# Down projection of a decoder's SwiGLU as seven block products instead of eight, one core of Trainium2

## The reference

```python
h = _rmsnorm(x, g_fp)
f = (jax.nn.silu(h @ w_g) * (h @ w_u)) @ w_d      # w_g, w_u: 1024 x 2816, w_d: 2816 x 1024
x = x + _rmsnorm(f, g_fq)
```

## Time and profile before

| | |
|---|---|
| median of 3 runs | 1484.61 us (1484.59 to 1484.89) |
| profiled execution | 1483.6 us, its span 1481.7 us |
| TensorE busy | 1462.8 us (99%), 10893 matmuls |
| VectorE, ScalarE, GpSimd busy | 801.7, 617.3, 267.4 us |
| DMA | 161.82 MB, mean 109 GB/s |
| down projection | from 1207.8 us on, 3 x 704 matmuls of 128x128 by 128x258 |

### The profile page before, as it was taken

One profiled execution on the slowest core, in us unless ns is written; L12 is line 12 of the kernel. 1 busy time (PEld: TensorE's weight loads), 2 busy tenths in 40 slices (PEclk: granted clock), 3 DMA queues, 4 the chain that ended last, 5 costly groups with the idle time before them and its releaser, 6 DMA issues.

```text
span 1481.7 us, 26774 instructions
## 1 busy us (share of the span) xinstructions
PE 1462.8 (99%) x10893; PEld 1416.5 (96%) x10893; DVE 801.7 (54%) x1441; ACT 617.3 (42%) x1223; POOL 267.4 (18%) x261
## 2 busy tenths in 40 slices
PE   7999999999999999999999999999999999999998
PEld 6999999999999999997799999999999999999997
DVE  7635676314334455755688765665765592235223
ACT  7336555335424521336675333333333363245222
POOL 2032221000000034330003323222322210002000
PEclk9999999999999999999999999999999999999999
DMA  7122323622203145135652223132332484345441
GB/s 228 29 58 67 110 77 101 178 83 77 72 29 90 29 125 163 58 129 190 204 154 80 88 84 105 62 99 73 94 98 75 139 270 120 108 125 184 123 134 58
DMA packets 203373, 161.82 MB, mean 109 GB/s; under 512 B 17306, under 2 KB 184482, under 8 KB 203252
## 3 DMA queue, kind: packets, MB, share of 16 engines
q1 hardware_dynamic: 199360, 148.00, 33.2%
q0 software_dynamic: 2720, 7.89, 1.7%
q10 hardware_dynamic: 1172, 4.23, 0.7%
HBM read 129.18 MB, written 30.92 MB: 108 GB/s over the span
## 4 chain that ended last, share of the span: by engine, by line
PE 92%; DVE 4%; ACT 2%; DMA 1%; issue 1%; DVEq 0%; ACTq 0%
PE bank L967 6%; PE bank L969 6%; PE bank L968 6%; PE bank L1583 6%; PE bank L1584 6%; PE bank L1585 6%; PE psAB L1511 3%; PE bank L1511 3%; PE psAB L1512 3%; PE psAB L1513 3%; PE bank L1512 3%; PE bank L1513 3%; PE psT L963 3%; PE bankC L1513 2%; PE bankC L1511 2%; PE bankC L1512 2%
## 5 line engine op out<-in xcount | busy, mean ns | idle before, releaser
L1583 PE MATMUL bank<-a_hi,s_hi 128*128 128x258 f32 x704 | 200.2, 284 | 0.2 <-DVE s_lo L2846 0.2
L1585 PE MATMUL bank<-a_hi,s_lo 128*128 128x258 f32 x704 | 198.7, 282 | 0.0
L1584 PE MATMUL bank<-a_lo,s_hi 128*128 128x258 f32 x704 | 198.7, 282 | 0.0
L967 PE MATMUL bank<-h_hi,w_hi 128*128 128x344 f32 x464 | 155.2, 335 | 3.0 <-DVE h_lo L2291 2.8
L969 PE MATMUL bank<-h_hi,w_lo 128*128 128x344 f32 x464 | 148.7, 320 | 0.0
L968 PE MATMUL bank<-h_lo,w_hi 128*128 128x344 f32 x464 | 148.6, 320 | 0.0
L1583 PEld LDWEIGHTS bank<-a_hi,s_hi 128*128 128x128 f32 x704 | 133.0, 189 | 0.6 <-issue 0.5
L1584 PEld LDWEIGHTS bank<-a_lo,s_hi 128*128 128x128 f32 x704 | 133.5, 190 | 0.0
L1585 PEld LDWEIGHTS bank<-a_hi,s_lo 128*128 128x128 f32 x704 | 132.9, 189 | 0.0
L2084 ACT ACTIVATE s_hi<-raw 128x512 fp32r<-128x512 f32 x126 | 78.7, 627 | 108.1 <-PE psAB L1513 99.1
L2846 DVE TENSOR_TENSOR s_lo<-rawd,s_hi 128x512 fp32r<-128x512 f32 x96 | 60.1, 645 | 109.3 <-ACT s_hi L2084 109.3
(11 more groups left out here) (586 smaller groups left out, 4283.3 us busy)
## 6 DMA issues: line engine op xcount, KB each, us to landing
rawd<-in_w_down SPq DMA_DIRECT2D x32, 704.0 KB, 6.5
raw<-in_w_gate SPq DMA_DIRECT2D x26, 512.0 KB, 4.0
raw<-in_w_up SPq DMA_DIRECT2D x26, 512.0 KB, 5.3
w_raw<-in_w_in SPq DMA_DIRECT2D x24, 512.0 KB, 4.1
w_raw<-in_w_out SPq DMA_DIRECT2D x24, 512.0 KB, 3.7
a_raw<-a_rows SPq DMA_DIRECT2D x20, 516.0 KB, 6.6
a_rows<-ab SPq DMA_DIRECT2D x18, 516.0 KB, 2.7
sx_raw<-in_w_in SPq DMA_DIRECT2D x18, 512.0 KB, 5.2
```

The source lines that it names most:

```text
L967: mm(out[:, 0:TG], w_hi[par][:, ws], hi[:, k, tgc[tg]], start=first, stop=False)
L1583: mm(out, hi[:, k, :], xh[:, k, :], start=(kg == 0 and k == 0), stop=False)
L1584: mm(out, hi[:, k, :], xl[:, k, :], start=False, stop=False)
L1585: ins = mm(out, lo[:, k, :], xh[:, k, :], start=False, stop=(k0 + k == NF - 1))
```

## The change

The down projection becomes a product of 2 by 2 blocks: the weights are cut in 1408 input and 512 output channels, the activations in 11 k tiles and 516 tokens. Seven products of 11 k tiles x 4 output tiles x 2 column halves replace the eight. The products are outermost, in the order A11, A12, S2, S3, S1, S4, A22 (named by the activation operand); all eight PSUM banks hold one product (4 output tiles x 2 halves of 258 columns), the first accumulates on into the second, and so do the third and fourth, and the fifth and sixth.

- Weights: one unit per k tile, 128x512. The sums of the four weight blocks are formed for each k tile by VectorE (`t_sums_of`) at the ends of eleven gate jobs (`T_JOBS`), from rows that SyncE loads (`t_load`), and stored to DRAM (`t_store`, 1 MB each); `down_load` then takes them from there.
- Activations: each of the four blocks is loaded whole, 2.9 MB, in three pieces. The sums S3, S2, S1, S4 are formed in place by VectorE (`a_sum`), between the splits of the first four products. High part and remainder of each k tile go through a ring of 8 places (`a_ring`).
- Results: ScalarE copies the first product (`dx_copies`), VectorE adds the later ones (`dx_sums`, `dx_last`); squares and gains as before on ScalarE, additions of squares on GpSimd.
- The last product runs over the first column half and then over the second, with the epilogue of the first token half in the first pass and more of it in the second.

```diff
-            for n in range(16):
-                down(n, 0)
-                if 9 <= n < 14:
-                    z_tile(Z_ORDER[n - 9])
-                down(n, 1)
-            pe.wait_ge(ev_s, 32)
+PRODUCTS = ("A11", "A12", "S2", "S3", "S1", "S4", "A22")
+KGROUPS = ((0, 3), (3, 1), (4, 1), (5, 1), (6, 1), (7, 1), (8, 3))
+LAST_GROUPS = ((0, 5), (5, 6))
+T_JOBS = (6, 7, 8, 10, 11, 12, 13, 14, 15, 17, 18)
...
+            def dx(x, g, m):
+                if g == 0:
+                    dx_free(x, m)
+                k0, kn = KGROUPS[g]
+                for k in range(k0, k0 + kn):
+                    n = KH * x + k
+                    if m == 0:
+                        pe.wait_ge(sp_lo, DOWN + n + 1)
+                        pe.wait_ge(al_s, n + 1)
+                    w = slot(DOWN + n, 0), slot(DOWN + n, 1)
+                    for s in range(2):
+                        ins = dx_three(dx_bank(m, s), w, k, a_part(n, 0)[:, dx_cols(s)], a_part(n, 1)[:, dx_cols(s)], m,
+                                       x in (0, 2, 4) and k == 0, x in (1, 3, 5) and k == KH - 1)
+                ins.then_inc(pe_ev, 1)
+            for x in range(6):
+                for g in range(len(KGROUPS)):
+                    for m in range(4):
+                        dx(x, g, m)
...
+            def t_sums_of(i):
+                b, n = tp[i % 2], 1 + 4 * i
+                dve.wait_ge(w_in_s[i % 2], 16 * (UNITS // 2) + 32 * (i // 2 + 1))
+                v.tensor_tensor(b[:, 4], b[:, 4], b[:, 1], ALU.subtract).then_inc(md_s, 1)
+                v.tensor_tensor(b[:, 1], b[:, 1], b[:, 0], ALU.subtract).then_inc(md_s, 1)
+                dve.wait_ge(md_s, n + 1)
+                v.tensor_tensor(b[:, 2], b[:, 4], b[:, 0], ALU.add).then_inc(md_s, 1)
+                dve.wait_ge(md_s, n + 3)
+                v.tensor_tensor(b[:, 3], b[:, 3], b[:, 2], ALU.subtract).then_inc(md_s, 1)
...
             for j in range(AHEAD, NJ):
                 job(j)
+                if j in T_JOBS:
+                    t_sums_of(T_JOBS.index(j))
+            SUM_AT = {(0, 9): ("S3", 1), (0, 11): ("S3", 2), (0, 13): ("S3", 0), (1, 5): ("S2", 0), (1, 8): ("S2", 1),
+                      (1, 10): ("S2", 2), (2, 5): ("S1", 0), (2, 8): ("S1", 1), (2, 10): ("S1", 2), (3, 5): ("S4", 0),
+                      (3, 8): ("S4", 1), (3, 10): ("S4", 2)}
+            for x in range(6):
+                for k in range(3, KH + 3):
+                    u, n = KH * x + k, KH * x + k + 2
+                    if u > 3:
+                        low(DOWN + u)
+                    if n >= RING and n < FULL:
+                        a_low(n)
...
+                    if (x, k) in SUM_AT:
+                        a_sum(*SUM_AT[x, k])
...
+                if x >= 2:
+                    for m in range(4):
+                        dx_sums(x, m)
...
+            def t_load(i):
...
+                if i >= 2:
+                    sp.wait_ge(kv_d, 16 * (52 + sum(j <= T_JOBS[i] - 2 for j in T_JOBS)))
+            def t_store(i):
+                sp.wait_ge(md_s, 1 + 4 * i + 4)
+                sp.wait_ge(kv_d, 16 * (52 + i))
+                sp.dma_start(t_d[P * i:P * i + P], tp[i % 2][:, 1:5, :]).then_inc(kv_d, 16)
```

More of the change, by code:

```diff
@@ L415, in build @@
[L415 to L418, removed]
+        rawd = [at(f"rawd{i}", [P, 4, 512], F32, X + 8192 * i)[0] for i in range(2)]
+        tp = [at(f"tp{i}", [P, 5, 512], F32, X + 10240 * i)[0] for i in range(2)]
+        AB = KH * 2 * NQ
@@ L419, in build @@
+        xr = [at(f"xr{i}", [P, D], F32, R[0] + 22720 + 4096 * i if i < 5 else R[0] + 4096 * (i - 5))[0] for i in range(8)]
+        xd = [at(f"xd{i}", [4, D], F32, R[0] + 12288 + 4096 * i)[0] for i in range(2)]
+        zt = [at(f"zt{i}", [P, NQ], F32, R[0] + (43200, 44256, 20480, 21536)[i])[0] for i in range(4)]
         tb = [(tA, tB, t1b), (t3a, t3b, t1a), (tA, tB, t1b)]
@@ L653, in z_x @@
         def z_x(t):
-            return xr[t % 4][:, :] if t < 8 else xd[t - 8][:, :]
+            return xr[t][:, :] if t < 8 else xd[t - 8][:, :]
         def cache(kk):
@@ L839, in store, with a_load @@
                 sp.dma_start(a_d[TILE[j]][:, cols], ab_of(j)[:, cols]).then_inc(a_out[j % 2], 16)
[L841 to L844, removed]
+            def a_load(block, p, landed):
+                first, h = {"A11": (0, 0), "A12": (KH, 0), "A21": (0, 1), "A22": (KH, 1)}[block]
+                to = a_blk[("A11", "A12", "A21", "A22").index(block)]
+                k, n = A_PIECES[p]
+                sp.dma_start(to[:, k:k + n, :], a_d[first + k:first + k + n, :, 2 * NQ * h:2 * NQ * h + 2 * NQ
+                                                    ].rearrange("f p c -> p f c")).then_inc(landed, 16)
             def stored(j):
@@ L885, in z_store @@
                 sp.dma_start(yp[t] if t < 8 else ys[4 * (t - 8):4 * (t - 8) + 4, :], z_x(t)).then_inc(z_out, 16)
-            done = [max(j for j in range(NJ) if 0 in HALVES[j] and TILE[j] < k + n) for k, n in KG]
             for j in range(2, NJ):
                 job_load(j)
[L890 to L898, removed]
                 if j == NJ - 2:
+                    sp.wait_ge(kv_d, 16 * (52 + KH))
                     down_load(0)
@@ L903, in _ @@
                     sp.wait_ge(pe_ev, event(NJ - 3, 6, 0))
-                    for kg in range(5):
-                        a_load(0, kg)
+                    for p in range(3):
+                        a_load("A11", p, a_in[p])
                     store(j - 2)
-                    a_load(1, 0)
-                    a_load(1, 1)
+                    for t in (0, 2, 3, 5, 8, 6, 7):
+                        sp.wait_ge(x1_out[STORED[t]], 16 * STORED.count(STORED[t]))
+                    a_load("A22", 0, a1_in)
                 else:
                     store(j - 2)
+                if j - 2 in T_JOBS:
+                    t_store(T_JOBS.index(j - 2))
+                if j in T_JOBS:
+                    t_load(T_JOBS.index(j))
                 if j == 3:
@@ new lines, in dx_last @@
+            def dx_last(c, k0, kn, m):
+                for k in range(k0, k0 + kn):
+                    n = FULL + KH * c + k
+                    if m == 0:
+                        if c == 0:
+                            pe.wait_ge(sp_lo, DOWN + FULL + k + 1)
+                        pe.wait_ge(al_s, n + 1)
+                    w = slot(DOWN + FULL + k, 0), slot(DOWN + FULL + k, 1)
+                    ins = dx_three(dx_bank(m, c), w, k, a_part(n, 0), a_part(n, 1), m, k == 0, k == KH - 1)
+                ins.then_inc(pe_ev, 1)
@@ new lines, in _ @@
+            for i in range(3):
+                low(DOWN + FULL + 8 + i)
+                a_low(FULL + 10 + i)
+            for i in range(3):
+                z_final(i)
+                a_low(FULL + 13 + 2 * i)
+                a_low(FULL + 14 + 2 * i)
+            for m in range(4):
+                dx_last(0, m)
+            for n in range(19, 22):
+                a_low(FULL + n)
+            for t in (3, 8, 4):
+                z_final(t)
+            dx_last(1, 0)
+            z_final(5)
@@ L3064, in _ @@
+            for m in (1, 2, 3):
+                dx_last(1, m)
+            for t in (6, 7, 9):
                 z_final(t)
```

594 lines of the change are left out of this document (370 added, 224 removed).

## The result

| | before | after |
|---|---|---|
| median | 1484.61 us | 1458.95 us of four runs (1458.24 to 1462.33) |
| profiled execution, its span | 1483.6, 1481.7 us | 1458.2, 1456.5 us |
| TensorE busy, matmuls | 1462.8 us, 10893 | 1432.9 us, 10633 |
| VectorE busy | 801.7 us | 881.2 us |
| DMA | 161.82 MB | 184.91 MB |

The ratio of the times is 0.9831, with a 95% interval of 0.9814 to 0.9848. The forecast was 1454.3 us, so 4.7 us of the gain that was worked out are missing. They were looked for stage by stage in the profiled execution. First the page of the changed kernel: the head, part 1, and of part 5 two groups of line 1601, the matmuls of the gate jobs (line 1511 before), with their idle time at the row's end. The head and part 1 answer to the earlier trace rows.

The account below looks back on a forecast made before the run. TensorE, busy 1462.8 of 1481.7 us, was taken as the bound. Terms -31.7 + 0 + 0 + 0.4 + 0.2 + 0.4 + 0.4 = -30.3 us gave 1453.3 profiled, 1454.3 us median; range 1452.0 to 1461.0 us.

Parts of the forecast that it names:

- The matmuls: Down projection: 264 of 2112 matmuls go at 0.11995 us each, price per matmul unchanged; -31.7 us.
- Changes of bank: Down projection: PSUM bank changes after every 3 matmuls; cost 0, at most 0.01 us at each of 616 changes.
- Weight sums at the ends of eleven gate jobs: Gate stage: four added VectorE sums per job take 2.8 us within 3.9 us of cover; cost 0, at most 10 us.
- rival 5: Down projection: granted clock falls to 1.2 GHz; half the stage's matmuls so would cost +90 us, 1544 us; chance 1%.
- Rival 1: Gate jobs: the weight sums stick out, TensorE idles behind u2; +5 us, 1459.3 us, at the bound 1464; chance 9%.
- the step on GpSimd: Gate jobs: GpSimd ends at 1017.87 us and stays idle during the new weight sums, so they are not slowed; cost 0.
- Start of the down projection: Third k tile's remainder waits on VectorE, +0.4 us; the 14.0 MB of loads and stores come in time, cost 0.
- The burst: Start of the down projection: 14.0 MB at 308 GB/s take 45 us, to 1233, before the second product at 1239.5; cost 0.
- Inside the products: Down projection: VectorE is 81% busy per product and keeps up; +0.2 us for all six changes of product.
- The end: After the last matmul: VectorE adds, then ScalarE squares while VectorE scales; +0.4 us.
- The four small terms: Down projection: its start +0.4, changes between products +0.2, epilogue transposes and sums +0.4, work after the last matmul +0.4 us.

Follow-up runs that it names:

- r1: The changed kernel run once more, unaltered, beside e1, e2 and e3 on one chip; 1460.66 us.
- e1: Changed kernel with the weight sums of jobs 8 and 15 moved away, `T_JOBS` now having 19 and 20 instead; 1453.25 us.
- e3: Changed kernel with the weight sums of jobs 8 and 15 on one column of 512, same instructions and DMAs at the same places; 1454.73 us.
- e4: e2 with four more VectorE operations in each group of weight sums, eight instead of four; 1484.49 us.
- e5: e2 with six more VectorE operations in each group of weight sums, ten instead of four; 1509.18 us.
- e2: Changed kernel with the weight sums of jobs 8 and 15 one job later, behind the one-half jobs 9 and 16; 1454.81 us.

## Why the prediction was right, and where it fell short

The direction and the mechanism of the gain were right, and the time lies inside the range; the sum was 4.9 us short for the profiled execution (1453.3 against 1458.2).

- **The matmuls:** right. 264 x 0.12 = 31.7 us, and the stage with all that follows it is 31.7 us shorter. That the two agree to 0.1 us is in part luck: the small terms below cancel.
- **Changes of bank:** right at 0. The spacing is 0.1203 us with a change after every three. The Trainium skill, "TensorE: Matmul & The Clock Gate", section "A second HAM failure mode: psum-queue depth-cycling", reports a loss of clock by short idle times where a bf16 kernel goes round the banks; here there are no such idle times, and the clock in the stage is 1.00 in the profiles of the changed kernel and of r1.
- **Weight sums at the ends of eleven gate jobs:** this is the step that failed. It placed the fourth product "behind six groups of 12 matmuls" and said cost 0. That is so for nine of the eleven jobs. Jobs 8 and 15 are followed by jobs with one half, as the description of the gate jobs says, and there it stands behind three groups. The trace of before showed the place: u2 ends at 908.29 and TensorE, after a distance of 0.37 instead of 0.12, starts at 908.35, so the cover was already used up and the whole 2.53 us had to come out as a pause. 2 x 2.53 = 5.1 us. e1 and e3 show that this is the cause. For the two-half jobs the working held: a cover of 1.1 us was reckoned, and e4 and e5 give 1.4.
- **The clock:** rival 5 said that TensorE "without a pause of its own gives no reason" for it. The pauses that the failed step brought gave one, in the gate stage: 1.4 us in the profiled execution, 2.9 in r1. In the stage that rival 5 meant, the clock is 1.00 in three of seven profiles of the new order (the changed kernel, r1, e1), and in the other four it falls once, without a pause ahead of it, for 1.6 us of time in e2. So the sentence does not hold without exception.
- **Rival 1** named the right symptom, idle time behind u2 and about 5 us, but the wrong mechanism: it asked for slower sums in all eleven jobs. A slow sum does occur, once in the profile (1.77 us), because the step on GpSimd was too favourable: it kept GpSimd's start at 1013.66, while the longer queue on SyncE moves it to 1016.33 in this job; in the whole gate stage GpSimd waits for a raw pair to land four times, 37.4 us in all, where it was twice and 8.7 us. The cover of 1.4 us absorbed the 1.1 us of it in the changed kernel; e4 shows what such sums cost when the cover is gone. The Trainium skill, "SBUF — State Buffer", section "Who interferes with whom", says that a VectorE instruction with two SBUF inputs and a GpSimd one that reads SBUF keep each other out; 1.77 us beside GpSimd against 0.68 and 0.72 alone agree with it.
- **Start of the down projection:** predicted +0.4, measured 0.60 - 0.12 = 0.5. The burst was in time: 375 GB/s in its window, and no wait where the second product starts. (The 45 us of loading from 1185.97 on end at 1231, not 1233 as the working has it; that changes nothing.)
- **Inside the products:** VectorE is busy 12.40 of 16.00 us, 78% against 81% worked out, and TensorE does not wait for it. The end is 1456.5 - 1446.80 = 9.7 us behind the last product, 9.5 before: +0.2 instead of +0.4. The four small terms, +1.4 together, were 0 in sum. Two of them were measured at +0.5 and +0.2, so -0.7 us came from elsewhere in the stage; where is open.

In numbers: -30.3 predicted; +5.1 for two pauses, +1.4 for the clock, -1.4 for the small terms; -25.2 us measured in the span.

## What to carry to other kernels

A cover that is worked out for one pass of a loop holds for that pass only: before work is hung on a list of jobs, go through the list and look for the job whose successor is shorter, since its cover is the smallest, and look in the trace for a place where the waiting engine is already late by a fraction of a microsecond. There every instruction that is added in front comes out whole. Where such work has slack in its order, as the table `T_JOBS` has, moving it costs nothing: e1 gained 7.4 us on the changed kernel measured beside it, and its edit is the eleven numbers of one table. A pause of the matmul engine should be priced above its own length, because the clock may fall behind it.

## What the runs showed of the hardware

- Behind pauses of 1.82 to 4.23 us, in a stream of matmuls that is otherwise full, a stretch at the lower clock followed in 17 of 20 cases over the profiles of the changed kernel, r1, e4 and e5; behind nine of 0.60 to 1.67 us in e4 and e5 in none. It came after TensorE was at work again, and lasted for 12 to 27 matmuls at 0.215 us instead of 0.12, so 1.1 to 2.6 us. Pauses of equal length, in one execution, went both ways (2.62 us in the changed kernel, 2.78 in e5).
- A VectorE sum of 128x512 with two inputs in SBUF takes 1.77 us beside GpSimd's sums and 0.68 alone, 2.6 times as long.
- In the last product the profiles of e2, e3, e4 and e5 each have one stretch at half clock, without a pause ahead of it; those of the changed kernel, r1 and e1, with the same instructions in the same order there, have none. In each of the four it begins ahead of the transposes, not behind them: in e2 the window from 1408.30 to 1409.60 shows a clock of 1.00 and that from 1409.90 on, where the transposes begin, 0.50. Shortly before, from 1406.4 to 1408.3, TensorE worked on one-column matmuls. Whether these are the cause was not tested.
